# Retention scores as split-precision passes over stacked key halves

## What is computed

```
scores  = einsum('bhnid,bhnjd->bhnij', q, k) * dmat      # per head, d = 64
y_inner = einsum('bhnij,bhnje->bhnie', scores, v)
y_cross = (q * xi) @ state_before_the_chunk
```

## Time and profile before

| | |
|---|---|
| median of 3 runs | 2824.47 us (2822.61 to 2825.63) |
| the profiled execution | 2824.45 us |
| its span in the trace | 2822.5 us |
| mean granted clock of TensorE | 0.994 of full |
| busy: TensorE, VectorE, ScalarE | 98%, 61%, 32% |
| the retention stage | about 1815 to 1886 us of the span |

### The profile page before, as it was taken

The page is one execution under the profiler, slowest core; times in us unless marked ns, Lnnn a source line. Parts: engine busy times, 40 slices in busy tenths (PEclk is TensorE's granted clock), DMA queues, the critical chain, the costliest instruction groups (busy, mean ns, idle before and its releaser), DMA issues.

```text
span 2822.5 us, 33195 instructions
## 1 busy us (share of the span) xinstructions
PE 2759.3 (98%) x12999; PEld 2299.0 (81%) x12999; DVE 1712.1 (61%) x1765; ACT 905.0 (32%) x841; POOL 7.0 (0%) x15
## 2 busy tenths in 40 slices
PE   6999999999999999999999899999999999999998
PEld 4778888888888888888888788888988888888886
DVE  6866757565665756665656843367665555555556
ACT  6631121211221212122112532355453333333333
POOL 0000000000000000000000000000000000000000
PEclk9999999999999999999999999999999999999999
DMA  9956545545555547676765343342445555555553
GB/s 310 300 192 200 180 144 164 150 152 171 156 163 149 178 143 255 198 256 196 234 193 193 107 117 97 120 111 84 135 164 194 188 185 192 192 185 187 192 184 130
DMA packets 408017, 496.83 MB, mean 176 GB/s; under 512 B 19091, under 2 KB 277513, under 8 KB 407177
## 3 DMA queue, kind: packets, MB, share of 16 engines
q1 hardware_dynamic: 407196, 493.10, 56.0%
q0 software_dynamic: 496, 2.63, 0.3%
q10 hardware_dynamic: 252, 0.10, 0.0%
HBM read 493.69 MB, written 2.10 MB: 176 GB/s over the span
## 4 chain that ended last, share of the span: by engine, by line
PE 85%; DVE 4%; ACT 3%; issue 2%; DMA 0%; ACTq 0%; DVEq 0%; SPq 0%
PE py L976 8%; PE py L978 8%; PE py L977 8%; PE pg L976 5%; PE pu L978 5%; PE pu L976 5%; PE pg L978 5%; PE pg L977 5%; PE pu L977 5%; PE py L1439 2%; PE py L1441 2%; PE py L1440 2%; ACT wh L573 2%; PE pg L1420 1%; PE pg L1422 1%
## 5 line engine op out<-in xcount | busy, mean ns | idle before, releaser
L1499 DVE TENSOR_TENSOR wl<-raw,wh 128x2048 fp32r<-128x2048 f32 x342 | 783.6, 2291 | 816.0 <-ACT wh L573 815.9
L573 ACT ACTIVATE wh<-raw 128x2048 fp32r<-128x2048 f32 x342 | 654.1, 1914 | 1345.0 <-PE py L978 488.6
L976 PE MATMUL py<-ah,wh 128*128 128x512 f32 x704 | 275.7, 392 | 1.1 <-DVE xy L1659 1.1
L978 PE MATMUL py<-ah,wl 128*128 128x512 f32 x704 | 274.2, 389 | 0.0
L977 PE MATMUL py<-al,wh 128*128 128x512 f32 x704 | 273.9, 389 | 0.0
L976 PE MATMUL pu<-hh,wh 128*128 128x512 f32 x656 | 255.9, 390 | 0.0
L976 PE MATMUL pg<-hh,wh 128*128 128x512 f32 x656 | 255.5, 389 | 0.0
L978 PE MATMUL pu<-hh,wl 128*128 128x512 f32 x656 | 255.3, 389 | 0.0
L978 PE MATMUL pg<-hh,wl 128*128 128x512 f32 x656 | 255.3, 389 | 0.0
L977 PE MATMUL pg<-hl,wh 128*128 128x512 f32 x656 | 255.2, 389 | 0.0
L977 PE MATMUL pu<-hl,wh 128*128 128x512 f32 x656 | 255.2, 389 | 0.0
(11 more groups left out here) (435 smaller groups left out, 4629.4 us busy)
## 6 DMA issues: line engine op xcount, KB each, us to landing
raw<-in_ffn_w_in SPq DMA_DIRECT2D x170, 1024.0 KB
chunk<-in_ada_w SPq DMA_DIRECT2D x189, 512.0 KB, 3.9
raw<-in_ffn_w_out SPq DMA_DIRECT2D x88, 1024.0 KB
raw<-in_ada_w SPq DMA_DIRECT2D x64, 512.0 KB
raw<-in_mix_w_in SPq DMA_DIRECT2D x30, 1024.0 KB
accc<-in_ada_w SPq DMA_DIRECT2D x35, 512.0 KB, 4.6
raw<-in_mix_w_out SPq DMA_DIRECT2D x16, 1024.0 KB
war<-in_ffn_w_in SPq DMA_DIRECT2D x16, 384.0 KB, 5.1
```

Source lines behind the costliest of these rows:

```text
L573: nc.scalar.activation(wh[:, slot % 2, :], raw[:, slot, :], ACT.Copy).then_inc(wh_ready, 1)
L976: mm(out_ap, w[0], xh_ap, start=first, stop=False, skip_group_check=True)
L978: return mm(out_ap, w[1], xh_ap, start=False, stop=last, skip_group_check=True)
L1499: tt(wl[:, slot % 2, :], raw[:, slot, :], wh[:, slot % 2, :].bitcast(F32), ALU.subtract).then_inc(wl_ready, 1)
```

## The change

The scores are made with reduced passes in place of an fp32 product. For each head a tile `rks` holds the rounded keys (64 channels) in one partition half and their low halves in the other, for all 512 keys. `rqh` holds the rounded queries twice, once in each partition half, and `rql` their low halves twice. One full-height matmul of `rks` by `rqh` gives high and low keys by high queries, a second by `rql` the same by low queries. Four blocks of keys make eight matmuls a head.

ScalarE makes the high halves (`ret_high`, three copies on 64 partitions), VectorE the low ones (`ret_low`, three subtractions on 64 partitions). Those of heads 0 and 1 are made ahead of the loop; then in turn h those of head h+2: on ScalarE between the high split and `decays(h+1)`, on VectorE between `weigh(h)` and `decay_arg(h+1)`. There are two buffers, so `ret_high(h)` waits until the scores of head h-2 are done. TensorE's scores wait for `ret_low`. No transfer is added or moved. The tiles lie in room that is free in this stage.

```diff
--- before.py
+++ after.py
@@ -172,6 +172,8 @@
     mixh = at("mixh", [P, 2 * HEADS, LAT], F32R, o_hh)
     mixl = at("mixl", [P, 2 * HEADS, LAT], F32R, o_hh + 16 * KB)
     yret = at("yret", [P, 2, HEADS * P], F32, o_hh + 24 * KB)
+    rks = at("rks", [P, 2, TOK], F32R, o_hl + 28 * KB)
+    rqh = at("rqh", [P, 2, LAT], F32R, o_e + 14 * KB)
     decay = at("decay", [P, 2, 4, LAT], F32, o_hh + 16 * KB)
     far = at("far", [P, 2, 4, LAT], F32, o_hl + 16 * KB)
     dback = at("dback", [P, 2, 2, LAT], F32, o_hl + 24 * KB)
@@ -208,6 +210,7 @@
     act = sm("act", [P, TOK])
     qnl = [at("qnl0", [P, 4, LAT], F32R, o_a + 4 * KB), at("qnl1", [P, 2, LAT], F32R, o_e + 14 * KB),
            at("qnl2", [P, 2, LAT], F32R, small[0])]
+    rql = at("rql", [P, 2, LAT], F32R, small[0])
     rms = sm("rms", [P, TOK])
     rope_t = sm("rope_t", [P, LAT])
     vt = sm("vt", [P, VROWS])
@@ -294,6 +297,7 @@
     swapped, rope_done = sem("swapped"), sem("rope_done")
     lnu_ready = sem("lnu_ready")
     darg_ready, decay_ready = sem("darg_ready"), sem("decay_ready")
+    reth_ready, retl_ready = sem("reth_ready"), sem("retl_ready")
     rs_done, rp_ready, ry_done, ry_free = sem("rs_done"), sem("rp_ready"), sem("ry_done"), sem("ry_free")
     yst_ready, ysd_ready, yn_ready, y_turned = sem("yst_ready"), sem("ysd_ready"), sem("yn_ready"), sem("y_turned")
     mixh_ready, mixl_ready, rg_ready, rgs_ready = sem("mixh_ready"), sem("mixl_ready"), sem("rg_ready"), sem("rgs_ready")
@@ -774,8 +778,20 @@
                     se.wait_ge(lnu_ready, 1)
                     nc.scalar.activation(lt[:, 1, :], lt[:, 0, :], ACT.Exp, scale=-1.0).then_inc(lnu_ready, 1)
 
+            def ret_high(h):
+                if h >= 2:
+                    se.wait_ge(rs_done, h - 1)
+                lo = (h % 2) * DK
+                nc.scalar.activation(rks[lo:lo + DK, h % 2, :], rk[lo:lo + DK, h // 2, :], ACT.Copy)
+                for o in (0, DK):
+                    ins = nc.scalar.activation(rqh[o:o + DK, h % 2, :], rq[lo:lo + DK, h // 2, :], ACT.Copy)
+                ins.then_inc(reth_ready, 1)
+
+            se.wait_ge(rope_done, 8)
+            ret_high(0)
             se.wait_ge(far_loaded, 16)
             decays(0)
+            ret_high(1)
             decays(1)
             for h in range(HEADS - 1):
                 if h == 3:
@@ -783,6 +799,8 @@
                 static_split(MIX0 + S_RG + h + 2)
                 if h == 4:
                     values_out(0)
+                if h + 2 < HEADS:
+                    ret_high(h + 2)
                 if 1 <= h:
                     decays(h + 1)
             se.wait_ge(rs_done, HEADS)
@@ -1221,11 +1239,12 @@
             def ret_scores(h):
                 if h >= 2:
                     pe.wait_ge(rp_ready, h - 1)
-                lo = (h % 2) * DK
+                pe.wait_ge(retl_ready, h + 1)
                 for j in range(4):
-                    ins = mm(py[2 * (h % 2) + j // 2][:, (j % 2) * LAT:(j % 2 + 1) * LAT],
-                             rk[lo:lo + DK, h // 2, j * P:(j + 1) * P], rq[lo:lo + DK, h // 2, :],
-                             start=(j % 2 == 0), stop=True, skip_group_check=True)
+                    b = py[2 * (h % 2) + j // 2][:, (j % 2) * LAT:(j % 2 + 1) * LAT]
+                    w = rks[:, h % 2, j * P:(j + 1) * P]
+                    mm(b, w, rqh[:, h % 2, :], start=(j % 2 == 0), stop=False, skip_group_check=True)
+                    ins = mm(b, w, rql[:, h % 2, :], start=False, stop=True, skip_group_check=True)
                 ins.then_inc(rs_done, 1)
 
             def ret_values(h):
@@ -1836,14 +1855,26 @@
                     ins = nc.vector.bn_aggr(ymv[:, k, h, :], yst[:, k, h, :])
                 ins.then_inc(yst_ready, 1)
 
+            def ret_low(h):
+                ve.wait_ge(reth_ready, h + 1)
+                lo = (h % 2) * DK
+                tt(rks[DK - lo:P - lo, h % 2, :], rk[lo:lo + DK, h // 2, :], rks[lo:lo + DK, h % 2, :].bitcast(F32), ALU.subtract)
+                for o in (0, DK):
+                    ins = tt(rql[o:o + DK, h % 2, :], rq[lo:lo + DK, h // 2, :], rqh[lo:lo + DK, h % 2, :].bitcast(F32), ALU.subtract)
+                ins.then_inc(retl_ready, 1)
+
             ve.wait_ge(far_loaded, 16)
             decay_arg(0)
+            ret_low(0)
             decay_arg(1)
+            ret_low(1)
             weigh(0)
             for h in range(HEADS - 1):
                 static_split(MIX0 + S_RG + h + 2)
                 if h:
                     weigh(h)
+                if h + 2 < HEADS:
+                    ret_low(h + 2)
                 if h >= 1:
                     ve.wait_ge(ry_done, h)
                     decay_arg(h + 1)
```

## The result

The changed kernel takes 2837.46 us (median of 5 runs, 2835.73 to 2840.58) against 2824.47: a ratio of 1.0049, 95% interval 1.0038 to 1.0060. It is 13.0 us slower. The forecast was 2837.8.

What follows compares the result with a forecast made beforehand. The prediction took a ring of VectorE and ScalarE in the retention heads as the bound: 10.4 us for ring and start plus 1.0 and 1.9 for clock falls, 13.3 in all, giving 2837.8 us, range 2831 to 2842.

Steps and rivals of the forecast that it cites:

- The ring: Retention heads: VectorE and ScalarE waiting on each other in turn, 9.12 us a head, forecast to become 10.80.
- The lower bound of 1.3: Least time `ret_low` would add per turn on VectorE, if its half-height subtractions overlap like full-height ones: 1.3 us.
- TensorE's loop: TensorE's repeat per retention head: 9.39 us, forecast to become 8.43 with scores 0.96 us shorter.
- The start: Start of the retention stage: TensorE stands 3.1 us for `ret_low(0)`, and gate slab 1 starts 2.1 us late.
- The sum to values 6: Retention stage up to head 6's values: start and five turns of 10.80 us, forecast +10.4 us.
- The clock at the end: Behind TensorE's stand before values 6: clock falls to half, slowing slab and values on the path, 1.9 us.
- the middle that I took of 1.5 and 2.3: Cost of a half-clock stretch behind the last stand, from two earlier falls costing 1.5 and 2.3 us: 1.9 us.
- the sum of 13.3: Whole forecast loss in the retention stage: 10.4 us, plus 1.0 and 1.9 for two clock falls.
- (a): Rival, retention stage: turns lengthen but TensorE's clock stays up or recovers at once, 2833 to 2835 us; chance 0.17.
- (b): Rival: the clock falls two or three more times or half-clocked stretches reach further, +17, 2841.5 us; chance 0.11.
- (c): Rival: VectorE's idle time absorbs the low halves, only the start is paid, +2.0, 2826.5 us; chance 0.07.
- (d): Rival: TensorE's loop sets the end, all eight heads give 0.96 us back, -7.7, 2816.8 us; chance 0.03.

Runs made afterwards that it cites:

- e3: The changed kernel, keeping all halves and their waits but computing the scores in fp32 as before: 2839.38 us.
- e1: The changed kernel with the three subtractions of `ret_low` made a second time for heads 2 to 7: 2845.71 us.
- e4: The changed kernel with `ret_low(h+2)` moved behind `decay_arg(h+1)` on VectorE: 2827.94 us.
- e11: The changed kernel with the two query subtractions of `ret_low` in the other order for even heads: 2838.29 us, one run.
- e2: The changed kernel with the three copies of `ret_high` made a second time for heads 2 to 7: 2838.24 us.
- e5: The changed kernel with VectorE's turn reordered to `weigh(h)`, `decay_arg(h+1)`, low split, `ret_low(h+2)`: 2819.99 us.
- e6: The changed kernel with both the VectorE order of e5 and the start of e8: 2815.52 us.
- e8: The changed kernel with only its start altered: both `ret_high` and `ret_low(0)` ahead of the distance table wait: 2835.58 us.
- e9: The changed kernel with gate slab 7 ahead of values 6 in TensorE's order: 2834.83 us.

## Why the prediction was right

**What bounds the stage.** Right. The ring of VectorE and ScalarE, not TensorE, sets the end: in e3 TensorE's time has no weight behind the start, in e1 that of VectorE has full weight, and in e4 its place decides.

**`ret_low`.** 1.68 us a turn were taken, the turns are 10.74 for odd and 10.83 for even heads, 1.62 and 1.71 more than 9.12. The lower bound of 1.3 was wrong for this order of halves. e11, in the better order, has 1.37 from L1861 to `decay_arg` and a turn that is still 1.50 longer than 9.12.

**`ret_high`.** Free in the loop, as said (e2). At the start it was rightly a link: `ret_low(1)` waited 0.6 us for it.

**TensorE's loop.** Taken as 8.43 us, it is 8.22 to 8.23 in e5. The scores are 0.95 us, as forecast; the rest is at the joints: as far as the timelines show, fp32 scores were preceded by a gap of about 0.1 us, and the first bank of values took 0.1 more behind them. In the changed kernel this is hidden, but it made e5 and e6 better than I expected.

**The start.** A stand of 3.1 us was forecast for TensorE, and 3.19 came.

**The sum to values 6.** From the first `decay_arg` to values 6 it was 1876.39 - 1815.48 = 60.9 us; it is 1889.54 - 1817.17 = 72.4. That is 11.5 more, for 10.4 of the ring and the start and 1.0 of the clock.

**The clock at the end.** Forecast at 1.9 us, it was 2.8: values 6 to up projections took 9.1 us and take 11.9. That is above the middle that I took of 1.5 and 2.3. The term was mis-sized, since the half level held until about 1895.6 (0.94 in the stretch from 1895), 6.1 us from the restart, where I had 3.4 to 5.2. The stage is thus 1.1 us longer than in the sum of 13.3. The difference of the medians, 13.0, is 1.4 under that of the profiled stages, within what runs scatter. The two offset each other: that the forecast was met to 0.3 us is luck, the mechanism and its size to some 1 us are not.

**What was not as told.** TensorE was to wait 2 us and more for `weigh` in every head from 3 on. It waited 0.3 us at head 4, 2.35 at head 5 and 6.3 at head 6, where about 8 were forecast, and at head 3 not for `weigh`, but 3.7 us in front of gate slab 4 for the copies of the first gates, which ScalarE makes behind its exponentials. In sum this is the same, for the ring rules either way. I had put only the copies' duration in the sum, and not asked who else waits for them.

**The rivals.** (a), the clock stays up, fell: it was at half behind each stand of 2.35 us and more in the changed kernel's stage. (b) was right that the clock falls more often, four times and not the two of the sum, but the two in the middle fall where TensorE has slack: (b) has the right sign, with 1 us and not with the 4 it needed. (c) would be e4's result, 2827.9 against the 2826.5 worked out, and belongs to another place of the three instructions. (d) is what e5 and e6 are: it takes the ring under TensorE's loop.

## What to carry to other kernels

Where two loops of nearly the same length run beside each other, shortening the slower one buys at most the difference, here 0.27 us a head; find the second loop before counting the gain, and take each new instruction's place as seriously as its price. The same three subtractions cost 9.5 us between `weigh` and `decay_arg` and nothing measurable a few instructions later. And an optimisation that loses may lack only its partner: reduced scores alone +13.0 us, the new order alone 0, both together -3.9 us, and with a better start -8.4 us.

## What the runs showed of the hardware

TensorE's granted clock was low behind short stands in this stage. It was at half behind the stands of 2.9 to 3.2 us at the start in all kernels that had them (0.66 in the 5 us from 1820, 0.60 in e5), and at full behind the one of 1.05 us in e6 and e8. Between these the length of the stand alone does not tell: values behind the stand of 2.35 us in the changed kernel are slow, 2.08 us for a bank that takes 1.16, and so they are in e3 behind one of 1.12 us, but those behind the 2.29 us of e9 take 1.16. The row of e3:

```profile
1877.79 2.08 PE L1256 MATMUL pa<-rv,decay 128*128 128x128 f32 x8 [1.12 <-DVE decay L1845]
```

The Trainium skill (TensorE: Matmul & The Clock Gate, "Why this matters for your kernels") warns of gaps above some 3 us; here less was sometimes enough.

Half-height VectorE subtractions that alternate between the partition halves follow each other without overlap: 0.70 us from start to start for 64x512, 0.44 for 64x256. Those that stay in one half overlap, as full-height ones do: 0.61 for 64x512.
